# First key block loaded during the gate tiles, and the last output transpose moved in among the output products

## What is computed

```python
hn = rmsnorm(h, norm_w[0])
proj = h @ w_in                          # one projection feeds all of it
gq, gk, gv, g_low, rw, gate = split(proj)
o_a = gla_chunked(gq, gk, gv, log_decay) # gated linear attention, chunks of 64 tokens
o_b = rwkv7_scan(r, decay, k, v, -kk, kk * a)
mean = jnp.mean(o_b, axis=-1, keepdims=True)
var = jnp.mean((o_b - mean) ** 2, axis=-1, keepdims=True)
o_b = (o_b - mean) * lax.rsqrt(var + RWKV_LN_EPS) * ln_w + ln_b
o_b = o_b + sum(r * k * r_k) * v         # the bonus
o = concatenate([o_a, o_b]) * silu(gate)
h = h + o @ w_out
```

## Time and profile before

| | us |
|---|---|
| median of 3 runs | 1271.71 (1271.07 to 1272.52) |
| the profiled execution's own time | 1268.04 |
| its span, first to last instruction | 1266.3 |
| `project0` in it | up to about 379.8 |
| `chunks0` | about 379.8 to 811.8 |
| `layer1_stage` | from about 811.8 |

### The profile page before, as it was taken

One profiled execution on the slowest core, in us unless ns is written; L12 is line 12 of the kernel. 1 busy time (PEld: TensorE's weight loads), 2 busy tenths in 40 slices (PEclk: granted clock), 3 DMA queues, 4 the chain that ended last, 5 costly groups with the idle time before them and its releaser, 6 DMA issues. The chain is left out here.

```text
span 1266.3 us, 32968 instructions
## 1 busy us (share of the span) xinstructions
PE 1173.1 (93%) x14856; PEld 889.3 (70%) x14856; DVE 503.9 (40%) x872; ACT 379.0 (30%) x851; POOL 385.5 (30%) x266
## 2 busy tenths in 40 slices
PE   5999999999995878999999897799999999999997
PEld 4677787888874767666656563498888875666786
DVE  5588884600002232332232222325552006887243
ACT  6334333411111223223223223311111117776111
POOL 2232323433212012222212112303333434554562
PEclk9999999999995688999999999899999998999999
DMA  6111114331305111112011002211111111111311
GB/s 239 33 39 46 34 34 135 115 116 50 116 0 204 37 46 52 31 46 70 28 45 54 20 20 93 86 34 50 47 39 47 50 34 34 35 35 36 148 50 67
DMA packets 50944, 78.91 MB, mean 62 GB/s; under 512 B 2544, under 2 KB 36096, under 8 KB 50432
## 3 DMA queue, kind: packets, MB, share of 16 engines
q1 hardware_dynamic: 50816, 76.98, 18.5%
HBM read 60.19 MB, written 16.78 MB: 61 GB/s over the span
## 5 line engine op out<-in xcount | busy, mean ns | idle before, releaser
L1461 PE MATMUL ps<-HNH,WH 128*128 128x512 f32 x736 | 289.9, 394 | 0.0
L1461 PE MATMUL ps<-HNL,WH 128*128 128x512 f32 x736 | 286.4, 389 | 0.0
L1461 PE MATMUL ps<-HNH,WL 128*128 128x512 f32 x736 | 286.4, 389 | 0.0
L1461 PEld LDWEIGHTS ps<-HNH,WH 128*128 128x128 f32 x736 | 138.2, 188 | 30.8 <-issue 2.7
L1461 PEld LDWEIGHTS ps<-HNH,WL 128*128 128x128 f32 x736 | 138.2, 188 | 30.4 <-issue 1.9
L1461 PEld LDWEIGHTS ps<-HNL,WH 128*128 128x128 f32 x736 | 138.2, 188 | 29.0
L1849 DVE CUSTOM_DVE_ANT_0 AR<-ps,GV,nsink 128x256 f32<-128x256 f32 x128 | 56.7, 481 | 98.8 <-PE ps L1659 97.8
L1045 PE MATMUL ps<-VQ,BK 128*128 128x512 f32 x128 | 69.7, 650 | 7.6 <-POOL BK L791 5.6
L1805 ACT ACTIVATE AR<-AR,nm 128x256 f32<-128x256 f32 x128 | 63.6, 500 | 19.4 <-DVE nm L1849 19.3
L1045 PE MATMUL ps<-WO,BK 128*128 128x512 f32 x128 | 64.9, 619 | 0.0
L1449 POOL CAST WH<-WA 128x1024 fp32r<-128x1024 f32 x16 | 19.1, 1191 | 136.8 <-PE ps L1461 106.9
(11 more groups left out here) (287 smaller groups left out, 2079.7 us busy)
## 6 DMA issues: line engine op xcount, KB each, us to landing
GV<-in_w1t SPq DMA_DIRECT2D x18, 512.0 KB, 3.4
AR<-in_x SPq DMA_DIRECT2D x16, 512.0 KB, 4.7
WA<-in_w0t SPq DMA_DIRECT2D x16, 512.0 KB, 3.4
RAW<-in_w0t SPq DMA_DIRECT2D x8, 512.0 KB, 3.7
bk_dram<-BK SPq DMA_DIRECT2D x1, 4096.0 KB, 17.9
BKS<-bk_dram SPq DMA_DIRECT2D x8, 512.0 KB, 5.6
h_dram<-AR SPq DMA_DIRECT2D x8, 512.0 KB, 3.4
AR<-h_dram SPq DMA_DIRECT2D x8, 512.0 KB, 7.1
```

The lines of the kernel that those rows point to most:

```text
L1461: last = pe.matmul(out, a, b, start=(k == 0 and i == 0), stop=(k == n - 1 and i == 2))
```

## The change

Key block 0 no longer has a tile of its own. `RAW` is kept alive through layer 0, and the two key buffers of the recurrence are its two halves: even key blocks (0, 2, 4, 6) in the second half, `RAW[:, 1, 0:T]`, odd ones in the first. The load of key block 0 moves from SP's queue in `chunks0` to the end of SP's queue in `project0`, behind two waits. Two of the mask loads change places. In turn 9 PE's transpose of `OB` moves from behind the eight products of block 6 to between the fourth and the fifth; in the other turns it stays where it was.

```diff
@@ trunk
+            RAW = sb("RAW", [P, 2, T + 1], ctx=layer0)
+            key_blocks = [RAW[:, 1 - i, 0:T].rearrange("p (a q t) -> p a q t", a=2, q=PAIRS) for i in range(2)]
+            bk_in0 = sem("bk_in0")
...
-                RAW = sb("RAW", [P, 2, T + 1], ctx=half1)
@@ project0, block.sync
+            sp.wait_ge(spilled[0], 16)
+            sp.wait_ge(gz_done, GP)
+            sp.dma_start(first_keys, spills[0][0]).then_inc(bk_in0, 16)
@@ chunks0
-    BK = [buf(f"BKS{i}", [P, 2, PAIRS, P]) for i in range(2)]
+    BK = key_blocks
...
             sp.dma_start(maska[:], maska_d).then_inc(s["masks_in"], 16)
+            sp.dma_start(maskb, maskb_d[:, 0]).then_inc(s["masks_in"], 16)
             sp.dma_start(maskd, maskd_d).then_inc(s["masks_in"], 16)
-            sp.dma_start(maskb, maskb_d[:, 0]).then_inc(s["masks_in"], 16)
...
             for n in spilled:
                 sp.wait_ge(n, 16)
-            load_keys(0)
             load_gla(0)
@@ chunks0, block.tensor
                 if ahead:
                     turn(PAIRS, lambda q: VT[:, q, tokens(n)])
                     join(n, 2)
+                if normed and not back:
+                    after(pe, "o_scaled", o)
+                    turn(PAIRS, lambda q: OB[:, q].rearrange("p a v -> p (a v)"))
                 output_products(o - 2, 1, (4,))
...
                 output_products(o - 2, 1, (7,))
-                if normed:
+                if normed and back:
                     after(pe, "o_scaled", o)
                     turn(PAIRS, lambda q: OB[:, q].rearrange("p a v -> p (a v)"))
```

More of the change, by code:

```diff
@@ L158, in trunk @@
                 project0(nc, sem, PS, HNH, HNL, WA, WBK, WRAW, WH, WL, parts, wup_sb, xw, gk_sb, gkup,
-                         spills, spilled, RAW, scanm, scan_d, AR, BK, VT, QK, GV, bdones, G, GG, small, w0t, col, const2_in,
+                         spills, spilled, key_blocks[0], bk_in0, RAW, scanm, scan_d, AR, BK, VT, QK, GV, bdones, G, GG, small, w0t, col, const2_in,
                          w_in, const_in, (par_sb, ident, istack), (par, ident_d, istack_d), (bdones_d, wup), ar_tiles,
@@ L164, in trunk @@
             with loop:
-                chunks0(nc, sb, sem, loop, banks, AR, VT, VQ, GV, G, GG, small, ident, istack, bdones, maska_d, maskd_d,
+                chunks0(nc, sb, sem, loop, key_blocks, bk_in0, banks, AR, VT, VQ, GV, G, GG, small, ident, istack, bdones, maska_d, maskd_d,
                         maskb_d, bk_tiles, col, spills, spilled, wout0, wo_in, x.rearrange("(t p) d -> p t d", p=P),
@@ L179, in project0 @@
 def project0(nc, sem, PS, HNH, HNL, WA, WBK, WRAW, WH, WL, parts, wup_sb, xw, gk_sb, gkup, spills,
-             spilled, RAW, scanm, scan_d, AR, BK, VT, QK, GV, bdones, G, GG, small, w0t, col, const_in, w_in, tables_in, tables,
+             spilled, first_keys, bk_in0, RAW, scanm, scan_d, AR, BK, VT, QK, GV, bdones, G, GG, small, w0t, col, const_in, w_in, tables_in, tables,
              tables_dram, late_dram, rows, x_dram, row_in, row_turn, rms, norm_sems):
@@ L594, in _, with chunks0 @@
                 dve.tensor_tensor(qk, qk, e, ALU.mult).then_inc(g_scaled, 1)
-def chunks0(nc, sb, sem, ctx, banks, AR, VT, VQ, GV, G, GG, small, ident, istack, bdones, maska_d, maskd_d, maskb_d,
+def chunks0(nc, sb, sem, ctx, key_blocks, bk_in0, banks, AR, VT, VQ, GV, G, GG, small, ident, istack, bdones, maska_d, maskd_d, maskb_d,
             SG, col, spills, spilled, w_dram, w_in, x_dram, row_in, row_turn, h1_dram, h1_out, wv1, wv_in, w1t, w1_in,
@@ L661, in chunks0 @@
     PAIR, STATE = banks[:, 0:2, :], banks[:, 2:4, :]
-    names = ("bk_in0 bk_in1 qk_in0 qk_in1 gv_in masks_in masks_set zeroed presets spare_zero "
+    names = ("bk_in1 qk_in0 qk_in1 gv_in masks_in masks_set zeroed presets spare_zero "
              "b_prod a_prod k_prod t_prod x_prod xt_prod x12_prod as_prod u_prod m_prod akv_prod rs_prod o_prod "
@@ L670, in chunks0 @@
     s = {n: sem("c_" + n) for n in names.split()}
+    s["bk_in0"] = bk_in0
     s.update(rms)
@@ L693, in _ @@
             sp.dma_start(maska[:], maska_d).then_inc(s["masks_in"], 16)
+            sp.dma_start(maskb, maskb_d[:, 0]).then_inc(s["masks_in"], 16)
             sp.dma_start(maskd, maskd_d).then_inc(s["masks_in"], 16)
-            sp.dma_start(maskb, maskb_d[:, 0]).then_inc(s["masks_in"], 16)
             def load_keys(d):
-                sp.dma_start(BK[d % 2][:], spills[0][d]).then_inc(s[f"bk_in{d % 2}"], 16)
+                sp.dma_start(BK[d % 2], spills[0][d]).then_inc(s[f"bk_in{d % 2}"], 16)
             def load_gla(d):
```

## The result

The changed kernel takes 1262.92 us (median of 18 runs, 1257.14 to 1271.89), the kernel before 1271.63 us in the 18 runs beside it (1266.20 to 1280.54). The ratio is 0.9935, 95% interval 0.9915 to 0.9955, so 8.3 us faster (5.7 to 10.8). The forecast was 1266.5 us with a range from 1264.2: faster, as forecast, but by more than the range held. Later, in a second set of runs, the same kernel gave 1266.68 us against 1270.34 and a ratio of 0.9953 (0.9930 to 0.9976), 6.0 us.

The account below looks back on a forecast made before the run. PE, busy 93% of the span, was taken as the bound, with time saved where it waits or runs at its lower clock. 3.43 + 2.43 - 0.7 = 5.2 us off 1271.7 gave 1266.5 us, range 1264.2 to 1270.2.

Parts of the forecast that it names:

- Part 2: Turn 9: with the transpose moved to 780.35, PE can go on at 785.47, 3.43 us sooner.
- part 3: Turn 9: the clock stays up after shorter idle time, block 7's four products take 3.67 us instead of 6.10, gaining 2.43.
- the clock falls all the same: Rival, turn 9: clock drops despite the shorter idle time, leaving 2.7 us of gain, 1269.0 us; chance 0.19.
- the edit does nothing: Rival, turn 9: block 7's products or layer 1 wait for something else, 0.7 us slower, 1272.4 us; chance 0.09.
- Part 1: Border: key block 0 loaded early, but DVE's mask work waits for POOL's scalings, first keep 0.7 us later, a loss.
- No meeting at all: Rival, border: POOL and DVE don't collide, early load gains 0.45 us, total 6.3 us, 1265.4 us; chance 0.17.
- The slower rival: Rival, recurrence: reading even key blocks from RAW's second half is slower, 14 us lost at twice the time, 1286; chance 0.05.
- The base: Whole kernel: the 5.2 us gain, derived from the profiled execution of 1268.04 us, taken off the runs' median 1271.7 us.

Follow-up runs that it names:

- pool_holds: Changed kernel, but POOL doesn't begin key block 0 before DVE's masks are made; ratio 0.9930 to the kernel before.
- key_only: Kernel before with key block 0 loaded early into RAW and masks swapped, turn 9's transpose left where it was; ratio 0.9977, 2.9 us faster.
- experiments of group 6: Changed kernel, and eye_first, each with the 4 MB output weight load moved from the border into turn 0; ratios 0.9945 and 0.9914 to the kernel before.
- late_load: Changed kernel with the load of key block 0 and the mask order put back to the border; ratio 0.9939 to the kernel before.
- placed_only: Kernel before with only the key blocks moved into RAW; ratio 0.9993.
- eye_first_late: eye_first with the load of key block 0 back at the border; ratio 0.9945 to the kernel before.
- turn_only: Kernel before with only turn 9's transpose moved amid the output products; ratio 0.9955, 5.7 us faster.
- eye_first: Changed kernel with DVE making the identities and RB before it waits for the masks; ratio 0.9941 to the kernel before.

## Why the prediction was right and wrong

**Part 2 and part 3 were right, part 3 to the tenth by luck.** Predicted 3.43 + 2.43 = 5.86 us; the trace has 35.06 - 29.23 = 5.83, and the edit alone measured 5.7 (1.9 to 9.5). The last products before took 5.11 to 6.61 us in four profiles, so the 2.43 us of part 3 could as well have been 1.4 or 2.9; both sides of the agreement come from the one profile in which it was 2.4. The idle time of 1.1 us, the clock at 1.00 and the 3.67 us (3.70) are as written. The rivals in which the clock falls all the same, or in which the edit does nothing, are out. The rule of the Trainium skill on transposes, "TensorE: Matmul & The Clock Gate", Part 4, would have made the fallen clock likely. The clock stayed up with the transposes in the middle, in every profile with this order.

**Part 1 was right in its mechanism and wrong in its size and sign.** POOL and DVE do meet, the keep came at 8.16 where 388.0 - 379.9 = 8.1 was written, and `pool_holds` takes the meeting away. No meeting at all was a rival and is out. But the term of the sum was a loss of 0.7 us, and `key_only` alone measured a gain of 2.9 us (a loss of 0.4 to a gain of 6.2). This is the term that failed, in two steps.

- "0.7 us later than before" went by one profile. Its keep at 7.36 was the earliest of six, so the loss at the keep is about 0.3 us.
- "The later keep then shifts PE's near products and all behind them." It doesn't. At the bonus, 13 us further, the three profiles of kernels with the early load and the meeting stand at 20.51, 20.49 and 20.49, the six with the border load at 20.53 to 21.57, 21.05 in the mean. The later keep has turned into a gain of 0.5 us: 0.8 us later at the keep, and the two waits for code behind it together 2.06 us instead of 3.42, which is 1.36 less. The prediction has no term for these waits. It noted that the loads behind key block 0 are issued 0.8 us sooner, and gave it no price. With 0.5 MB less in front of them, the output weights landed at 18.7 instead of 20.2. The two waits sum to 2.0 to 2.1 us in the three profiles with the early load and the meeting, and to 2.3 to 3.4 in the six with the border load. The experiments of group 6 show this link with the large load moved. That it is the 0.5 MB that shortens the waits here is an inference: `late_load`, with the weights at 20.1, comes close (2.29 us, bonus 20.53).

One more reading was loose: "DVE's operations there read two tiles from SBUF" doesn't hold for the four `RB` operations, which read one tile and one value per partition. They were stretched all the same, 1.27 us instead of 0.87.

**What stays open.** From the bonus to turn 9 the changed kernel's two profiles took 373.2 and 375.1 us, those of the kernel before 375.9 and 375.3. `key_only` took 372.6 there and `pool_holds` 376.0, `placed_only` 375.7, `late_load` 374.5, `eye_first_late` 375.5 and `turn_only` 383.1, so the early load isn't told from chance. The rest of `key_only`'s gain, if it is real, lies in there, and I can't name a place for it. With the 5.8 us of turn 9 and 0.5 us at the border the traces account for 6.3 us. The first set of runs had 8.3 (5.7 to 10.8), the second 6.0 (3.1 to 8.9). The second lies inside the range, and the two intervals overlap, so what is missing may be no more than the scatter of the runs; that isn't shown either. It doesn't save the term: at the bonus its sign was wrong.

**The slower rival** (keys read from an odd address) is out: `placed_only` measured 0.9993. Its first L843 takes 1.99 us for 32 products after the idle time, as L840 did before (1.98), and the first products of every later block take 1.10 us (once 1.20), as L840's do at the full clock. The 1.98 us from which this rival was sized was the time at the low clock.

**The base.** I took the profiled execution's gain off the median of three runs, 1271.7; over all its later runs the medians are 1270.3 to 1271.8. That step was good.

## What to carry to other kernels

A wait that is removed at a point where large loads run is worth only what the next wait leaves, and the next one may be code: look for "issue" before PE's rows and at the instruction queue beside the loads. Cost every load that moves up or down in a queue, not only the one that the edit names. A term below a microsecond needs more than one profile of the kernel before: here the same instruction began 7.36 or 7.88 us after the same point.

## What the hardware showed unasked

- **Code is not free.** PE fetches 16 KB every 4 us in the median in the recurrence (most 3.4 to 6.4 us apart), and is put down as idle for "issue" for 34 to 42 us between the keep and turn 9, in every profile. That is about a tenth of the stretch, and more than it waits there for all other engines together (9 to 16 us). The Trainium skill, "Runtime: NRT & Kernel Launch", section "Instruction fetch mechanics", calls the cost of crossing such a block mostly hidden. In this stretch of small matmuls some 30 of the 84 were not, with waits of 1.2 us in the mean and up to 3.2.
- **A fetch beside a large load comes late:** at the border the first one starts 6.1 to 6.7 us after the keep with the 4 MB beside it and 3.6 to 3.7 without, and in turn 0 two of them are 5.9 to 6.8 us behind the one before instead of 3.4 to 5.5.
- **Two operations of VectorE in a row can be stretched by one of GpSimd after another:** the four `RB` operations took 2.62 us in `eye_first`, 1.27 in the changed kernel, 0.87 to 0.89 alone.

```profile
381.31 2.62 DVE L1275 TENSOR_SCALAR RB<-bdones,par 128x128 f32<-128x128 f32 x4
384.02 1.05 DVE L1277 TENSOR_TENSOR near<-RR 128x192 int32<-128x192 int32 x1
```

- **Layer 1 has two usual lengths**, about 451 us and about 454.5 us, in kernels of either kind (two of the fourteen profiles lie between, at 452.3 and 452.5): 454.36 and 451.01 in the two profiles of the kernel before, 451.39 and 454.55 in those of the changed one. The windows from 1032 to 1064 us show the difference: the clock is 0.84 in the long ones (before, first profile; changed kernel, second) and 0.95 in the short ones. Here are the two profiles of the kernel before:

```profile
1032.00:1064.00 32.00, 28.88 (x175) 20.67 (x175) 13.70 (x53) 15.14 (x49) 13.85 (x11) 0.84 0.06 17
```

```profile
1032.00:1064.00 32.00, 28.88 (x191) 21.09 (x191) 13.79 (x55) 16.24 (x51) 14.94 (x12) 0.95 0.06 17
```

  PE is busy for the same 28.88 us in both, with 175 products in the one and 191 in the other; the low stretch is 10.3 us long in the one and 3.4 us in the other, and 3 us of the whole time go with it. What decides between them no run shows. The projection drifts in the same way: it ends 379.7 to 385.3 us into the span. The clock records show no low clock in it in the six profiles where it ends by 381.1, and 10.2 us of low clock in the two where it ends at 385.0 and 385.3. Both are part of why single runs of one kernel lie 14 us and more apart.
